# First tap of the state-space branch's convolution: written by GpSimd where VectorE wrote it

## The reference

```python
def _causal_conv(x, buf, w, b):
    T = x.shape[1]
    xp = jnp.concatenate([buf, x], axis=1)
    out = xp[:, 0:T] * w[0]
    for j in range(1, CONV_W):
        out = out + xp[:, j:j + T] * w[j]
    return out + b, xp[:, -(CONV_W - 1):]
...
    qk, mconv1 = _causal_conv(jnp.concatenate([mq, mk], axis=-1), mconv0, p['m_conv_w'], p['m_conv_b'])
    qk = jax.nn.silu(qk)
...
    xbc, sconv1 = _causal_conv(xbc, sconv0, p['s_conv_w'], p['s_conv_b'])
    xbc = jax.nn.silu(xbc).astype(f32)
    xs = xbc[..., :S_INNER].reshape(Bsz, T, S_GROUPS, S_HPG, S_HEADDIM)
    Bm = xbc[..., S_INNER:S_INNER + S_GROUPS * S_STATE].reshape(Bsz, T, S_GROUPS, S_STATE)
```

## Time and profile before

| | before |
|---|---|
| median of 3 executions | 1375.01 us (1373.16 to 1376.38) |
| the profiled execution: its own time | 1379.06 us |
| the profiled execution: span | 1377.3 us |
| busy: PE, DVE, ACT, POOL | 1280.8, 764.8, 625.9, 207.2 us |
| mean granted clock of TensorE | 0.972 of full speed |

### The profile page before, as it was taken

How to read it: one execution, slowest core, us unless ns; L and a number is a source line. 1 busy time by engine, 2 the same in 40 slices (tenths; PEclk the granted TensorE clock), 3 DMA queues, 4 the chain that set the end, 5 groups by cost and what they waited for, 6 DMA issues and landing times.

```text
span 1377.3 us, 22618 instructions
## 1 busy us (share of the span) xinstructions
PE 1280.8 (93%) x9088; PEld 1162.5 (84%) x9088; DVE 764.8 (56%) x1324; ACT 625.9 (45%) x1085; POOL 207.2 (15%) x363
## 2 busy tenths in 40 slices
PE   6799999996999889989999989999999979999997
PEld 3699999994997767768998778788899959999997
DVE  1544445335785446746379666865466564555443
ACT  3433334324567536545355654554563344333433
POOL 3000000001550312111023232321410010000010
PEclk9899999998999999999999999999999989999998
DMA  9856666876343487883764445473335463444551
GB/s 303 217 184 216 214 201 191 232 234 214 124 123 108 170 296 258 279 279 120 205 199 135 124 139 155 138 212 118 114 95 166 141 214 123 153 153 134 143 144 46
DMA packets 258862, 241.56 MB, mean 175 GB/s; under 512 B 8607, under 2 KB 242479, under 8 KB 258710
## 3 DMA queue, kind: packets, MB, share of 16 engines
q1 hardware_dynamic: 249262, 211.03, 50.4%
q0 software_dynamic: 9024, 28.91, 6.1%
q10 hardware_dynamic: 472, 0.17, 0.1%
HBM read 209.88 MB, written 30.21 MB: 174 GB/s over the span
## 4 chain that ended last, share of the span: by engine, by line
PE 56%; DVE 5%; ACT 4%; issue 3%; DMA 1%; POOL 1%; ACTq 0%; DVEq 0%; POOLq 0%
PE bank L770 49%; PE aux L770 6%; ACT w_hi L1465 1%; ACT arena L1451 1%; DVE w_lo L2043 1%; PE aux L767 1%; DVE arena L2202 1%; PE bank L767 1%; DMA arena<-in_state_mlstm_C 0%; DMA out_p_C<-arena 0%; ACT L1832 0%; ACT arena L1832 0%; DVE arena L2534 0%; DVE arena L2577 0%; POOL arena L740 0%
## 5 line engine op out<-in xcount | busy, mean ns | idle before, releaser
L2043 DVE TENSOR_TENSOR w_lo<-ring,w_hi 128x1024 fp32r<-128x1024 f32 (+1 forms) x264 | 336.2, 1274 | 439.8 <-ACT w_hi L1465 439.6
L1465 ACT ACTIVATE w_hi<-ring 128x1024 fp32r<-128x1024 f32 (+1 forms) x264 | 289.5, 1097 | 559.9 <-PE bank L770 554.9
L770 PE MATMUL bank<-u_hi,w_hi 128*128 128x320 f32 x1536 | 275.4, 324 | 19.9 <-ACT w_hi L1465 19.7
L770 PEld LDWEIGHTS bank<-u_hi,w_hi 128*128 128x128 f32 x1536 | 241.2, 196 | 34.7 <-issue 31.5
L770 PE MATMUL bank<-u_lo,w_hi 128*128 128x320 f32 x1536 | 259.5, 312 | 0.0
L770 PE MATMUL bank<-u_hi,w_lo 128*128 128x320 f32 x1536 | 256.8, 310 | 0.0
L770 PEld LDWEIGHTS bank<-u_lo,w_hi 128*128 128x128 f32 x1536 | 237.2, 191 | 0.0
L770 PEld LDWEIGHTS bank<-u_hi,w_lo 128*128 128x128 f32 x1536 | 234.1, 188 | 0.0
L600 POOL TENSOR_TENSOR arena<-arena 128x320 f32<-128x320 f32 x24 | 21.0, 873 | 634.0 <-ACT arena L1477 621.2
L767 PE MATMUL aux<-ident,arena 128*128 128x128 f32 (+6 forms) x404 | 62.3, 280 | 21.7 <-ACT arena L1451 9.3
L767 PEld LDWEIGHTS aux<-ident,arena 128*128 128x128 f32 (+6 forms) x404 | 45.7, 145 | 35.5 <-issue 17.0
(11 more groups left out here) (354 smaller groups left out, 1508.8 us busy)
## 6 DMA issues: line engine op xcount, KB each, us to landing
ring<-in_w_in SPq DMA_DIRECT2D x52, 1024.0 KB, 5.4
ring<-in_ff_w SPq DMA_DIRECT2D x44, 1024.0 KB, 5.5
ring<-in_ada_w SPq DMA_DIRECT2D x36, 1024.0 KB, 6.9
ring<-in_ff_w SPq DMA_DIRECT2D x32, 704.0 KB, 4.8
arena<-in_state_mlstm_C SPq DMA_DIRECT2D x32, 512.0 KB, 4.3
out_s_C<-arena POOLq DMA_DIRECT2D x32, 512.0 KB, 4.9
ring<-in_w_pa SPq DMA_DIRECT2D x8, 1024.0 KB, 7.3
arena<-in_state_ssm SPq DMA_DIRECT2D x32, 256.0 KB, 3.6
```

The costliest lines, as they stand in the source:

```text
L770: return nc.tensor.matmul(dst, lhs, rhs, start=first, stop=last)
L1465: nc.scalar.activation(w_hi[v.split_no % 2][:, 0:v.kc, :], panel_part(v), ACT.Copy).then_inc(S["hi_done"], 1)
L2043: V.tensor_tensor(w_lo[r][:, 0:v.kc, :], panel_part(v), w_hi[r][:, 0:v.kc, :].bitcast(FP32), ALU.subtract)\
```

## The change

In xbc units POOL writes the first tap too, with the weights and bias columns of that branch, after the same two waits as in qk units. DVE no longer writes it and waits for `tap_done` in every unit. The other three taps, the copies into `tails` and everything else stay.

```diff
@@ conv_side (GpSimd) @@
-                if u.name == "qk":
-                    pool.wait_ge(S["hist_put"], c + 1)
-                    if c >= 4:
-                        pool.wait_ge(S["conv_silu"], c - 3)
-                    nc.gpsimd.tensor_scalar(acc[:, c % 4, 0:CONVW], padded[:, r, 0:CONVW], par[:, u.own + 120:u.own + 121],
-                                            par[:, u.own + 104:u.own + 105], ALU.mult, ALU.add).then_inc(S["tap_done"], 1)
+                pool.wait_ge(S["hist_put"], c + 1)
+                if c >= 4:
+                    pool.wait_ge(S["conv_silu"], c - 3)
+                a, w_col, b_col = (acc, 120, 104) if u.name == "qk" else (acc2, 240, 216)
+                nc.gpsimd.tensor_scalar(a[:, c % 4, 0:CONVW], padded[:, r, 0:CONVW], par[:, u.own + w_col:u.own + w_col + 1],
+                                        par[:, u.own + b_col:u.own + b_col + 1], ALU.mult, ALU.add).then_inc(S["tap_done"], 1)
@@ conv (VectorE) @@
                 a, p = accs[:, c % 4, 0:CONVW], padded[:, r, :]
-                if u.name == "qk":
-                    dve.wait_ge(S["tap_done"], c + 1)
+                dve.wait_ge(S["tap_done"], c + 1)
                 c = own
-                if u.name != "qk":
-                    ch.link(V.tensor_scalar(a, p[:, 0:CONVW], par[:, c + w_col:c + w_col + 1], par[:, c + b_col:c + b_col + 1], ALU.mult, ALU.add))
```

## The result

| | before | after |
|---|---|---|
| median, measured side by side | 1375.70 us (1372.12 to 1379.64, 6 executions) | 1386.11 us (1381.95 to 1392.88, 6 executions) |
| ratio | | 1.0078, 95% interval 1.0055 to 1.0102 |
| profiled execution: time, span | 1379.06, 1377.3 us | 1384.56, 1382.8 us |
| busy: DVE, POOL | 764.8, 207.2 us | 755.8, 231.3 us |
| executions of the study: mean | 1379.44 us, ± 0.6 (142) | 1386.27 us, ± 1.2 (27) |

The change makes the kernel slower, by 0.4% to 0.8%: the three comparisons of it gave 1.0078, 1.0041 and 1.0052, with intervals that reach from 1.0019 to 1.0102. The forecast was 1376.8 us and no measurable change. Part of that miss is the base.

What follows compares the result with a forecast made beforehand. The chain was taken as mostly PE, with DVE's first tap in it at six places. Terms 0.7 + 0.2 + 0.75 + 0.1 = 1.75 us on 1375.01 gave 1376.8 us, range 1373.5 to 1380.0.

Steps and rivals of the forecast that it cites:

- What bounds the kernel: Whole kernel: the chain that ended last is mostly PE, DVE holds 5%; moving taps matters only where DVE is in it.
- The six places: Stream's last unit, i = 0 of phases 0, 1, 2 and i = 1 of phases 1, 2: the whole stake.
- No progress under DVE: POOL's tap stands still while DVE runs an instruction reading two SBUF tensors; on-time wait +0.22 us, late unit +0.12.
- The stream, +0.7: Stream's last unit: `w_lo` about 0.6 us late plus 0.12, so second tap 0.7 us later; bounds +0.2 to +1.0.
- Phase 0: Unit i = 0 of phase 0: everything shifts together, the pattern of an on-time unit, +0.2 us.
- the +0.1 for places taken to be covered: Units i = 2 and 3, and i = 1 of phase 0: spare time nearly hides waits of 0.2; +0.1 us in all.
- Phases 1 and 2, +0.75: Phases 1 and 2: +0.2 us each at i = 0 on time, +0.16 each at i = 1 with DVE late.
- The sum: All places: 0.7 + 0.2 + 0.75 + 0.1 = 1.75 us on a median of 1375.01, giving 1376.8 us.
- The tap is ready in time: First rival, at the six places: DVE does not wait, 3.0 us gained, 1372.0 us; chance 0.08.
- POOL holds up DVE: Second rival, stream and phases: POOL's work takes the ports first, +0.25 us per DVE tap pair; sum 4.35, 1379.4 us; chance 0.16.
- The picks come late: Third rival: POOL's L718 comes 0.5 to 0.9 us later, at worst 0.3 us in nine units, 1379.5 us; chance 0.04.
- Nothing is lost: Last rival: the waits fit into spare time, the time stays within 0.5 us of 1375.0; chance 0.12.

Runs made afterwards that it cites:

- a fill: Sixteen unneeded transposes in PE's wait at the stream's end: in the changed kernel 1382.88 and 1382.43 us (1.0013, 1.0035), in the kernel before 1378.43 us (0.9995).
- the delay without POOL: Kernel before, all xbc taps on DVE; in the stream's last unit DVE writes the first tap again, then half of it once more: 1383.28 us (1.0019).

## Why the prediction was wrong

**What bounds the kernel: right.** The six places held all of the stake but 0.19 us. All lasting steps of the matmul starts that the change made stand at them and at i = 1 of phase 0, and a kernel with 12 taps elsewhere is as fast as before.

**No progress under DVE: right.** In the stream 1.77 us lie between `w_lo` and the second tap, as in the earlier trace rows, and the tap of 742.23 took 1.80 us for a work of 0.63. The Trainium skill (SBUF — State Buffer, section "Who interferes with whom") says that a VectorE instruction with two inputs in SBUF and a GpSimd instruction that reads SBUF exclude each other; the trace agrees with its 1.77 us, and with it that moving the tap gives no overlap here.

**The stream, +0.7: the step itself right (0.75), its price wrong.** This is the step that failed. The prediction put the longer wait into the sum as its length alone, at full clock: what the clock does behind it stood at nothing, with no reason given. The measured place costs 0.75 + 1.58 = 2.33 us, since in all three traces of the changed kernel the granted clock is 0.50 for some 3 us behind the wait. None of the eight traces in which PE waited 1.0 to 2.0 us there had that, nor any of the three with a fill; of six with 2.52 or 2.77 us, four did. In the four the half clock begins 2.75 to 2.81 us behind the start of the wait, although they came to the place up to 4.4 us apart. That a longer wait there can be followed by the half clock is shown, by the delay without POOL and by the fill. Why two of the traces with 2.52 us were spared is not: they had reached the place earlier (by 0.41 and 1.96 us against before, the three of after 1.00 to 5.44 later), which fits an effect of the moment, and was not tried apart.

**Phase 0: 0.32 against 0.2 and a share of 0.1.** i = 0 cost 0.13 by the steps, a little under the 0.2 forecast. i = 1 cost 0.19, and it was in the +0.1 for places taken to be covered. The row of that place had not been read: in the trace of before DVE ends what PE waits for next 0.06 us ahead of PE's start at 758.63:

```profile
758.30 0.27 DVE L2579 SCALAR_TENSOR_TENSOR arena<-arena 64x128 f32<-64x128 f32 x1
...
758.63 0.87 PE L770 MATMUL bank<-arena 128*64 128x256 f32 x8
```

Units i = 2 and 3, whose rows had been read, were covered, as forecast: i = 2 without a step, i = 3 with the 0.22 us that are made up for.

**Phases 1 and 2, +0.75: 0.93.** i = 0 cost 0.22 each, as forecast. i = 1 cost 0.24 and 0.25 and not 0.16. The rows of after in phase 1 show the mistake:

```profile
818.51 1.21 DVE L2043 TENSOR_TENSOR w_lo<-ring,w_hi 128x1024 fp32r<-128x1024 f32 x1
820.37 1.19 DVE L2199 SCALAR_TENSOR_TENSOR arena<-arena,par 128x344 f32<-128x344 f32 x2 [0.65 <-POOL arena L620]
```

1.86 us, the wait of a unit on time, and not the 1.77 of a late one: DVE comes 0.22 late, but so does everything that releases POOL, since the bank that ACT copies was also filled 0.22 later. A delay that all share makes nobody late.

**The sum.** Waits 2.0 us against 1.75 forecast; that part held. The clock behind the stream, 1.6 in the profiled executions, was missing. Of the measured 6.8 us (± 1.3) the granted clocks of the executions give 3.1 (± 1.3) to the half clock at the most, which holds these 1.6, and 3.7 (± 0.9) to everything else, against the 2.0 us of waits. So some 1.7 us beside the clock have no place in the traces and stay open. A tap on POOL away from the path is excluded as a wait that could be their source. Where the other 1.5 us of half clock fall can't be said from three traces: they hold 47.8 to 51.2 us of half clock ahead of 701 us, where nothing was changed, and the two of before 41.0 and 44.4, so part of it may be chance.

**The rivals.** *The tap is ready in time*: no; L2199 waited at all six. *POOL holds up DVE*: no; pairs stay at 1.19 us, and a `w_lo` that starts 0.17 us behind a tap (742.23 and 742.40) still takes 1.22. The part of the rule on which this rival rests, that whoever starts first keeps the ports to its end, is not seen at these places: a tap that begins under the end of one DVE instruction gives way to the next. *The picks come late*: they waited for PE, and PE did not wait for them. They also had more room than the prediction read: 822.46 + 1.25 = 823.71 is 1.9 us ahead of 825.60, not 1.3. On POOL, after:

```profile
751.48 0.29 POOL L718 CAST w_hi_rest<-w_lo_rest 64x128 fp32r<-64x128 f32 x1 [1.34 <-PE aux L770]
```

*Nothing is lost*: no. The chance of 0.20 for slower stood for the most part on the second and third rival, and the slower that came was neither.

**The base.** The sum was set on a median of three executions, 1375.01, of a program whose mean over 142 is 1379.44: 4.4 us of the 9.3 by which the forecast missed. The profiled execution, at 1379.06, was the better base and was discounted for lying above the median. With it the same sum gives 1380.8, still below what was measured.

## What to carry to other kernels

Moving an instruction to an idle engine saves nothing where the instruction in front of it keeps the new engine from working, as `w_lo` did here; look at what the new engine runs beside, not at how idle it is. Price a longer PE wait twice: its length, and the half clock that may stand behind it; where a wait grows to 2.5 us as here, a few matmuls that nobody reads are a cheap way to learn which of the two one pays. Where half-clock stretches come and go between executions, three executions are no base for a 0.2% forecast, and the start of one and the same matmul in two traces tells a shift of 0.1 us that no median does.

## What the hardware showed that was not expected

The same program, up to the same matmul at 701 us, was up to 4.4 us apart in three executions of the changed kernel (1.00, 1.87 and 5.44 us later than before), and 9.7 over all kernels (the earliest 4.30 us sooner), while the 39 us of the stream behind it, without a half clock, repeated to 0.01 us. Stretches at the 1.2 GHz level come and go ahead of 701 us from one trace to the next: 37.6 us of them in the trace that got there at 697.56, 51.2 in the one at 706.44. They don't make the whole of the spread, since another with 51.2 us was there at 702.00. A wait of PE that grew by 0.75 us, from 1.77 to 2.52, cost 2.33 us with what stood behind it. And a half clock can cost less than its absence: where PE ran at full clock to the matmul of 982.44, it waited 2.43 us there, had the half clock behind the wait instead, and was 2.1 us later by 1040.
